# Turning and moving feed-forward blocks off TensorE in a streaming-encoder block: VectorE 32x32 turns plus transfers

## The chip, the cores and the metric

The kernel runs on one core of one Trainium2 chip. The metric is the device time of one execution in microseconds (us). Three executions of the kernel before took 1131.97, 1132.44 and 1132.74 us, median 1132.44 us. Engines are called by their names in the profile: PE (TensorE matmul), PEld (TensorE weight load), DVE (VectorE), ACT (ScalarE), POOL (GpSimd), SP (SyncE, which issues most transfers).

## What is computed

One layer of a hybrid encoder on 256 tokens of width 2048, all float32: a retention group and a state-space group side by side, an output projection added to the residual, and a dense feed-forward block of inner width 5632.

```python
h = rmsnorm(x, norm_mix_g)
proj = h @ w_in                                  # 2048 x 5120
y_ret = retention_group(q, k, v, g, ...)         # 1024 columns
y_ssm = s5_group(u, ...)                         # 1024 columns
x = x + concatenate([y_ret, y_ssm]) @ w_out      # 2048 x 2048
h = rmsnorm(x, norm_ffn_g)
x = x + (silu(h @ w_gate) * (h @ w_up)) @ w_down # 2048 x 5632, twice, and 5632 x 2048
return rmsnorm(x, norm_final_g)
```

## The kernel before, in words

**Chunks.** All weights are read from memory once, in chunks of 256 x 512 values (512 KB), numbered through the whole program: `N_IN` = 80 chunks of `w_in`, 8 of the state-space gate, 16 + 16 of `w_out` (starting at `RET0` and `SSM0`), 16 of the first `w_gate` and `w_up` column block (starting at `FFN0` = `SSM0` + 16), and then from `LOOP0` = `SSM0` + 32 on ten turns of `TURN` = 24 chunks each: 8 chunks of the next gate column block, 8 of the next up block, 8 of `w_down` for the block that the turn before computed. Nine turns are a hardware loop, the tenth is written out. A last piece works off the final `w_down` chunks.

**The pipeline of a chunk n.** SP loads it into one of four `raw` slots, once `low(n - 4)` on DVE has finished with that slot. ACT copies it to `w_hi` (`high(n)`, a rounded value that TensorE takes at full rate), once PE has finished chunk n - 4. DVE computes `w_lo = raw - w_hi` (`low(n)`). PE then multiplies three times, hi by hi, hi by lo and lo by hi, 12 matmuls of 512 columns (`column_chunk`). So `raw` and `w_hi`/`w_lo` each hold four chunks, and DVE and ACT run up to four chunks ahead of PE. Each engine's order is written out by hand: after `low(n)` or `high(n)` an engine runs what `side(n)` lists for that n, and what `turn` lists for chunk c of a turn (c from 4 to 27 on ACT and DVE, since they are four ahead, 0 to 23 on PE and SP).

**Activations must be turned.** The left operand of each matmul has its contraction index on the partitions, while results have tokens there. So two kinds of data are turned by 128x128 blocks. In both, PE turned eight blocks into PSUM at a time, ACT copied them out as the hi part, DVE computed the lo part.

- The residual `x2`, in four column blocks c of 512 (`h2_transposes(c)` on PE after chunk `SSM0 + 5 + 4c`, `h2_high(c)` and `h2_low(c)` at `SSM0 + 9 + 4c`). A column block is complete when `out_col_ssm(c)` has run on DVE at `SSM0 + 7 + 4c`; the semaphore `cols_added` says so, and PE waits for it before it turns the block.
- The feed-forward block `ff_act` (256 tokens x 512), eleven of them. `ff(count, ...)` on DVE makes it at c = 19 of a turn, for use in the next turn; `ff_transposes` on PE turned it after c = 7, `ffT_high` on ACT and `ffT_low` on DVE at c = 11; the `w_down` chunks, c = 16 to 23, use it. The eleventh block is turned near the end by the same function, into `ffE`.

**Other waits in a turn.** `down_col(0)` on DVE, at c = 21, adds the first 512 output columns to `x2` and raises `cols_added`; PE's chunk c = 20 waits for it, since it reuses those PSUM banks. `silu` on ACT, at c = 11, overwrites `ff_act`.

Of the kernel before, what the change touches and what calls it, by code (L numbers as in the profile page):

```python
# [28 lines left out]
P = 128  # L29
# [97 lines left out]
SQUARES_AT = 8  # L127

# [6 lines left out]
ACT_PART = slice(0, 768)  # L135


def build(nc, A, out):
# [20 lines left out]
    with ctx:  # L159
# [18 lines left out]
        m = overlay([("qT", [P, HEADS, SEQ], F32)], [("u_tok", [P, TOK, 1024], F32)],  # L178
                    [("cosA", [P, HALF, NCH], F32), ("sinA", [P, HALF, NCH], F32)])
        qT, u_tok, cosA, sinA = m["qT"], m["u_tok"], m["cosA"], m["sinA"]  # L180
        ret = qT
        m = overlay([("u_loc", [P, GROUPS, NCH], F32)],
                    [("ffE_hi", [P, 4, SEQ], F32R), ("ffE_lo", [P, 4, SEQ], F32R)])
        u_loc, ffE_hi, ffE_lo = (m[k] for k in ("u_loc", "ffE_hi", "ffE_lo"))
        m = overlay(
# [91 lines left out]
            "ffT_mm ffT_hi_ready ffT_lo_ready fin_sq gain_done fin_ready fin1_ready last_mm"  # L277
        ).split()
        S = {n: sem(n) for n in names}
# [66 lines left out]
        def _(sp):  # L346
            def load(n, src, turn=None):
# [8 lines left out]
                sp.dma_start((raw4 if glu else raw2)[:, slot], src).then_inc(d_raw[slot], 16)  # L356

# [39 lines left out]
            for n in range(LOOP0):  # L397
                before(n)
                if n:
                    load(n, chunk_source(n))  # L400

            sp.wait_ge(S["ret_ready"], 2)
            sp.dma_start(g_final[:], A["g_final"]).then_inc(d_gfin, 16)
            with sp.Fori(0, FG - 1) as j:
                for c in range(TURN):
# [7 lines left out]
                    load(LOOP0 + c, src.rearrange("(b p) n -> p b n", p=P), turn=j)  # L413
            for c in range(GRP):
# [11 lines left out]
        def _(act):  # L426
# [63 lines left out]
            def side(n):  # L490
# [143 lines left out]

                c, r = divmod(n - (SSM0 + 9), 4)
                if r == 0 and 0 <= c < 4:
                    h2_high(c)
                    x2_square(c)
# [41 lines left out]
            def h2_high(c):  # L680
                act.wait_ge(S["h2_mm"], c + 1)
                for k in range(4):
                    kb = 4 * c + k
                    src = ps[:, 4 + 2 * (c % 2) + k // 2, SEQ * (k % 2):SEQ * (k % 2 + 1)]
                    nc.scalar.activation(h2(kb, 0), src, ACT.Copy, scale=vec[:, V_FFN + kb:V_FFN + kb + 1]
# [73 lines left out]
        def _(dve):  # L759
# [300 lines left out]
            def h2_low(c):  # L1060
                for k in range(4):
# [3 lines left out]
                    src = ps[:, 4 + 2 * (c % 2) + k // 2, SEQ * (k % 2):SEQ * (k % 2 + 1)]  # L1065
                    gain_low(h2(kb, 1), src, V_FFN + kb, h2(kb, 0)).then_inc(S["h2_lo"], 1)
# [44 lines left out]
            def side(n):  # L1111
# [287 lines left out]
        def _(pe):  # L1399
# [252 lines left out]
            def side(n):  # L1652
# [32 lines left out]
                if r == 0 and 0 <= c < 4:  # L1685
# [63 lines left out]
            def turn(j, final=False):  # L1749
                for c in range(TURN):  # L1750
# [132 lines left out]
```

## Time and profile before

| What | Value |
|---|---|
| median of three runs | 1132.44 us |
| the profiled execution, its time | 1131.68 us |
| its span, first to last instruction | 1129.9 us |
| granted TensorE clock, mean | 0.998 |
| PE busy | 1116.9 us (99%) |
| DVE busy | 714.4 us (63%) |
| ACT busy | 532.6 us (47%) |
| transfers | 224.81 MB, mean 199 GB/s |

The profiled execution's time is 1.8 us above its span, and 0.76 us below the median of the three runs. Busy shares are means over a program whose first third (projection, retention, state space) is more crowded on DVE than the feed-forward part, which begins at about 391 us and is a regular stream of chunks.

### The profile page before, as it was taken

Reading aid. Unit: us, or ns where it says so; the run is one execution under the profiler, and the core shown is the slowest. Engines: PE = TensorE matmul, PEld = TensorE weight load, DVE = VectorE, ACT = ScalarE, POOL = GpSimd, SP = SyncE. Lnnn points to the kernel's source line nnn. Section 1 sums busy time; section 2 is a strip of 40 time slices with the busy share of each in tenths; the row PEclk is TensorE's granted clock in tenths of the full one; section 3 lists DMA queues with packets and bytes.
Section 4 is the critical chain, followed back from the end, with each engine's and each line's share of the span. In section 5 each row is a group of like instructions: output and inputs, shape, how many; then the busy total and the mean of one; then the engine's idle time right before and its main releaser. Section 6 shows DMA issues by size and latency. Waiting matters only on the chain.

```text
span 1129.9 us, 15159 instructions
## 1 busy us (share of the span) xinstructions
PE 1116.9 (99%) x5618; PEld 925.9 (82%) x5618; DVE 714.4 (63%) x783; ACT 532.6 (47%) x640; POOL 88.3 (8%) x130
## 2 busy tenths in 40 slices
PE   9999999999999999999999999999999999999996
PEld 7878778888988888888888888888888888888885
DVE  7999998566765645464555546455554645556466
ACT  7569444346734553444343343444444343443443
POOL 7120234320000000000000000000000000000000
PEclk9999999999999999999999999999999999999999
DMA  9883788855666576666665666666566666656652
GB/s 362 286 234 115 205 249 257 230 170 153 232 212 197 171 219 201 189 190 186 192 197 186 189 190 195 187 189 195 187 192 186 192 190 193 188 186 201 187 187 93
DMA packets 115095, 224.81 MB, mean 199 GB/s; under 512 B 8432, under 2 KB 13936, under 8 KB 114416
## 3 DMA queue, kind: packets, MB, share of 16 engines
q1 hardware_dynamic: 110832, 214.05, 61.1%
q0 software_dynamic: 3808, 9.31, 3.3%
q10 hardware_dynamic: 416, 0.92, 0.2%
q8 instruction: 26, 0.43, 0.2%
q14 instruction: 13, 0.11, 0.0%
HBM read 218.09 MB, written 5.11 MB: 198 GB/s over the span
## 4 chain that ended last, share of the span: by engine, by line
PE 84%; DVE 10%; DMA 2%; issue 1%; ACT 1%; POOL 0%; SPq 0%; POOLq 0%; DVEq 0%; ACTq 0%
PE ps L1415 70%; DVE w_lo L778 4%; PE ps L1440 3%; PE ps L1433 3%; PE ps L1437 3%; DMA raw<-in_w_in 2%; PE ps L1649 1%; DVE wb L905 1%; DVE wb L903 1%; DVE wb_t L904 1%; PE ps L1718 1%; PE ps L1719 1%; PE ps L1720 1%; PE ps L1548 0%; DVE cl_t L978 0%
## 5 line engine op out<-in xcount | busy, mean ns | idle before, releaser
L778 DVE TENSOR_TENSOR w_lo<-raw,w_hi 128x1024 fp32r<-128x1024 f32 x384 | 468.0, 1224 | 383.4 <-ACT w_hi L442 382.3
L442 ACT ACTIVATE w_hi<-raw 128x1024 fp32r<-128x1024 f32 x383 | 406.0, 1061 | 563.2 <-PE ps L1415 456.2
L1415 PE MATMUL ps<-w_hi,actA_hi 128*128 128x512 f32 x416 | 112.4, 392 | 0.0
L1415 PE MATMUL ps<-w_hi,actA_lo 128*128 128x512 f32 x416 | 111.2, 389 | 0.0
L1415 PE MATMUL ps<-w_lo,actA_hi 128*128 128x512 f32 x416 | 111.2, 389 | 0.0
L1415 PE MATMUL ps<-w_lo,h2B_hi 128*128 128x512 f32 x352 | 94.1, 389 | 0.0
L1415 PE MATMUL ps<-w_hi,h2B_hi 128*128 128x512 f32 x352 | 94.1, 389 | 0.0
L1415 PE MATMUL ps<-w_hi,h2B_lo 128*128 128x512 f32 x352 | 94.1, 389 | 0.0
L1415 PEld LDWEIGHTS ps<-w_hi,actA_lo 128*128 128x128 f32 x416 | 78.1, 188 | 16.3
L1415 PEld LDWEIGHTS ps<-w_lo,actA_hi 128*128 128x128 f32 x416 | 78.1, 188 | 16.2
L1415 PEld LDWEIGHTS ps<-w_hi,actA_hi 128*128 128x128 f32 x416 | 77.1, 188 | 15.3
L1415 PE MATMUL ps<-w_hi,ffT_hi 128*128 128x512 f32 x320 | 85.6, 389 | 0.0
L1415 PE MATMUL ps<-w_lo,ffT_hi 128*128 128x512 f32 x320 | 85.5, 389 | 0.0
L1415 PE MATMUL ps<-w_hi,ffT_lo 128*128 128x512 f32 x320 | 85.5, 389 | 0.0
L1415 PEld LDWEIGHTS ps<-w_hi,h2B_hi 128*128 128x128 f32 x352 | 66.1, 188 | 13.7
L1415 PEld LDWEIGHTS ps<-w_hi,h2B_lo 128*128 128x128 f32 x352 | 66.1, 188 | 13.7
L1415 PEld LDWEIGHTS ps<-w_lo,h2B_hi 128*128 128x128 f32 x352 | 66.1, 188 | 13.7
L1415 PEld LDWEIGHTS ps<-w_hi,ffT_lo 128*128 128x128 f32 x320 | 60.1, 188 | 12.5
L1415 PEld LDWEIGHTS ps<-w_lo,ffT_hi 128*128 128x128 f32 x320 | 60.1, 188 | 12.5
L1415 PEld LDWEIGHTS ps<-w_hi,ffT_hi 128*128 128x128 f32 x320 | 60.0, 188 | 12.4
L1381 POOL TENSOR_TENSOR ss<-ss 128x2 f32<-128x2 f32 x1 | 0.2, 193 | 711.4 <-ACT y1T L746 711.4
L1109 DVE TENSOR_TENSOR x<-ps,x 128x1024 f32<-128x1024 f32 x40 | 48.7, 1218 | 0.0
(271 smaller groups left out, 1265.0 us busy)
## 6 DMA issues: line engine op xcount, KB each, us to landing
raw<-in_w_gate SPq DMA_DIRECT2D x88, 512.0 KB, 3.7
raw<-in_w_up SPq DMA_DIRECT2D x88, 512.0 KB, 3.7
raw<-in_w_down SPq DMA_DIRECT2D x88, 512.0 KB, 3.7
raw<-in_w_in SPq DMA_DIRECT2D x79, 512.0 KB, 5.3
raw<-in_w_out SPq DMA_DIRECT2D x32, 512.0 KB, 3.9
k_tab<-k_scratch POOLq DMA_DIRECT2D x64, 64.0 KB, 4.3
raw<-in_ssm_w_glu SPq DMA_DIRECT2D x8, 512.0 KB, 3.6
x_tok<-in_x_tok SPq DMA_DIRECT2D x2, 1024.0 KB, 8.4
```

What stands on the lines that cost most here:

```text
L442: nc.scalar.activation(w_hi[:, s % SPL], raw[:, s % RAW], ACT.Copy).then_inc(S["high_done"], 1)
L778: tt(w_lo[:, s % SPL], raw[:, s % RAW], w_hi[:, s % SPL].bitcast(F32), ALU.subtract).then_inc(S["low_done"], 1)
L903: tt(o, of_groups(b_re, b, LOC - 1), of_powers(pr, b, 1, LOC - 1), ALU.mult)
L904: link(tt(t, of_groups(b_im, b, LOC - 1), of_powers(pi, b, 1, LOC - 1), ALU.mult))
L905: tt(o, o, t, ALU.add).then_inc(S["wb_ready"], 1)
L1109: tt(cols, ps[:, b0:b0 + 2], cols, ALU.add).then_inc(S["cols_added"], 1)
L1415: ins = mm(ps[:, banks + t], blocks[k][kind == 1][:, tok], w[:, s, at], start=first and kind == 0 and k == 0, stop=last and kind == 2 and ...
L1433: mm(ps[:, banks + t], blocks[k][0][:, tok], w_hi[:, s, at], start=first and k == 0, stop=False)
L1437: mm(ps[:, banks + t], blocks[k][1][:, tok], w_hi[:, s, at], start=False, stop=False)
L1440: ins = mm(ps[:, banks + t], blocks[k][0][:, tok], w_lo[:, s, at], start=False, stop=last and k == 1)
L1649: ins = tr(ps[:, bank + k // 2, at:at + P], ff_act[:, t, P * k:P * (k + 1)], ident[:])
L1718: mm(o, w_hi[:, n % SPL, at], hi, start=first, stop=False)
```

## The change

Twelve of the fifteen sets of eight PE turns are replaced: the ten `ff_transposes(j + 1)` inside the turns, and `h2_transposes(0)` and `(1)`. The last feed-forward block and residual columns 2 and 3 stay on PE. In the replaced cases DVE turns each 32x32 square in place (`turned_blocks`, two instructions of 128x512, one per 128 tokens, into `ff_turned` or `x2_turned`), and SP then issues sixteen transfers, one per pair (a, b) of 32-partition groups, each 32 partitions x 2 x 128 values (32 KB), which put the squares where a full turn has them (`ff_moved`, `x2_moved`). ACT and DVE read these buffers instead of PSUM. In a turn the sixteen transfers go out in pairs behind the loads of c = 5 to 12; for a residual column in groups of 6, 5 and 5 behind the loads of `SSM0 + 11 + 4c` and the next two.

Times in the order change with it: `ffT_high` moves from c = 11 to c = 15, `ffT_low` from c = 11 to c = 16, `turn_blocks` is new at c = 20, and `h2_high`/`h2_low` of the four columns go from `SSM0` + 9, 13, 17, 21 to `SSM0` + 14, 18, 18, 21.

```diff
+MOVED = 16 * 16
+COLS_MOVED = 2
+PAIRS = [(a, b) for a in range(4) for b in range(4)]
+H2_AT = (SSM0 + 14, SSM0 + 18, SSM0 + 18, SSM0 + 21)
...
+            def move(pairs, turned, moved, landed):
+
+                for a, b in pairs:
+                    sp.dma_start(moved[32 * b:32 * b + 32, :, a].rearrange("p t k j -> p t (k j)"),
+                                 turned[32 * a:32 * a + 32, b].rearrange("p t k j -> p t (k j)")).then_inc(landed, 16)
...
+                c, r = divmod(n - (SSM0 + 11), 4)
+                if 0 <= c < COLS_MOVED and r < 3:
+                    if r == 0:
+                        sp.wait_ge(S["turned"], c + 1)
+                    move(PAIRS[(0, 6, 11)[r]:(6, 11, 16)[r]], col_turned[c % 2], col_moved[c % 2], d_cols[c])
...
+                    if 5 <= c < 13:
+
+                        if c == 5:
+                            sp.wait_ge(S["turned"], j + (COLS_MOVED + 1))
+                        move(PAIRS[2 * (c - 5):2 * (c - 4)], ff_turned, ff_moved, d_moved)
...
             def h2_high(c):
-                act.wait_ge(S["h2_mm"], c + 1)
+                if c < COLS_MOVED:
+                    act.wait_ge(d_cols[c], MOVED)
+                else:
+                    act.wait_ge(S["h2_mm"], c + 1 - COLS_MOVED)
...
             def ffT_high(count):
-                act.wait_ge(S["ffT_mm"], count)
-                nc.scalar.activation(ffT_hi[:].rearrange("p (a b) s -> p a (b s)", a=2), ps[:, 4:6], ACT.Copy
+                act.wait_ge(d_moved, count * MOVED)
+                nc.scalar.activation(turned_view(ffT_hi[:]), moved_view, ACT.Copy
                                      ).then_inc(S["ffT_hi_ready"], 1)
...
                     if c == GRP + SPL - 1:
+
+                        act.wait_ge(S["turned"], j + (COLS_MOVED + 1))
+                        silu(j * TURN + (LOOP0 + GRP))
+                    if c == GRP + SPL + 3:
                         ffT_high(j + 1)
-                        silu(j * TURN + (LOOP0 + GRP))
...
+            def turn_blocks(count, moved):
+
+                dve.wait_ge(S["ff_ready"], count)
+                if moved is not None:
+                    dve.wait_ge(d_moved, moved)
+                else:
+                    dve.wait_ge(d_cols[2 * (COLS_MOVED - 2)], MOVED)
+                turned_blocks(ff_turned, ff_act)
...
+            def turned_blocks(to, x):
+
+                for t in range(TOK):
+                    last = nc.vector.transpose(to[:, :, t].rearrange("p b k j -> p k b j"),
+                                               x[:, t].rearrange("p (k b j) -> p k b j", k=4, b=4))
+                last.then_inc(S["turned"], 1)
...
+                    if not last and c == 2 * GRP + 4:
+                        turn_blocks(j + 2, (j + 1) * MOVED)
...
-                if r == 0 and 0 <= c < 4:
+                if r == 0 and COLS_MOVED <= c < 4:
                     h2_transposes(c)
...
                         pe.wait_ge(S["cols_added"], j * 4 + 8)
-                        ff_transposes(j + 1)
```

**Place 1, DVE around the residual columns.** `x` in the rows is `x2`; the L1085 rows (with the change L1135) are `out_col_ssm(2)` and `out_col_ssm(3)`, the L778 rows (L828) are `low`, the L792 rows (L842) are `h2_low`. Before, from `out_col_ssm(2)` at `SSM0 + 15` to `out_col_ssm(3)` at `SSM0 + 19`:

```order
L1085 SCALAR_TENSOR_TENSOR x<-ps,rstd,x 128x512 x2
L778 TENSOR_TENSOR w_lo<-raw,w_hi 128x1024 x2
L792 SCALAR_TENSOR_TENSOR h2B_lo<-ps,x_in,h2B_hi 128x256 x4
L778 TENSOR_TENSOR w_lo<-raw,w_hi 128x1024 x2
L1085 SCALAR_TENSOR_TENSOR x<-ps,rstd,x 128x512 x2
```

With the change, from `h2_low(0)` at `SSM0 + 14` to `low(SSM0 + 21)`:

```order
L842 SCALAR_TENSOR_TENSOR actA_lo<-ff_moved,x_in,actA_hi 128x256 x4
L828 TENSOR_TENSOR w_lo<-raw,w_hi 128x1024
L1135 SCALAR_TENSOR_TENSOR x<-ps,rstd,x 128x512 x2
L828 TENSOR_TENSOR w_lo<-raw,w_hi 128x1024 x3
L842 SCALAR_TENSOR_TENSOR actA_lo<-x_moved,x_in,actA_hi 128x256 x4
L842 SCALAR_TENSOR_TENSOR h2B_lo<-ps,x_in,h2B_hi 128x256 x4
L828 TENSOR_TENSOR w_lo<-raw,w_hi 128x1024
L1135 SCALAR_TENSOR_TENSOR x<-ps,rstd,x 128x512 x2
L828 TENSOR_TENSOR w_lo<-raw,w_hi 128x1024 x2
```

Between `low(SSM0 + 18)` and `out_col_ssm(3)` there now stand eight small instructions and one `low`, where there was one `low`: column 1's lo part came here from `SSM0 + 13`, column 2's from `SSM0 + 17`.

**Place 2, DVE inside the loop, c = 19 to 21 of a turn.** Before:

```order
L778 TENSOR_TENSOR w_lo<-raw,w_hi 128x1024
L1091 ISA
L1093 SCALAR_TENSOR_TENSOR ff_act<-ps,rstd,ff_act 128x512 x2
L777 REGISTER_ALU
L778 TENSOR_TENSOR w_lo<-raw,w_hi 128x1024
L777 REGISTER_ALU
L778 TENSOR_TENSOR w_lo<-raw,w_hi 128x1024
L1106 ISA
L1109 TENSOR_TENSOR x<-ps,x 128x2x512
```

With the change:

```order
L828 TENSOR_TENSOR w_lo<-raw,w_hi 128x1024
L1141 ISA
L1143 SCALAR_TENSOR_TENSOR ff_act<-ps,rstd,ff_act 128x512 x2
L827 REGISTER_ALU
L828 TENSOR_TENSOR w_lo<-raw,w_hi 128x1024
L1150 REGISTER_ALU
L1168 STREAM_TRANSPOSE ff_turned<-ff_act 128x4x4x32 x2
L827 REGISTER_ALU
L828 TENSOR_TENSOR w_lo<-raw,w_hi 128x1024
L1181 ISA
L1184 TENSOR_TENSOR x<-ps,x 128x2x512
```

The two block turns stand between the `low` of c = 20 and that of c = 21, ahead of `down_col(0)` (L1109, now L1184), for which PE waits.

**Place 3, SP's queue at the residual columns.** Before, the rows are 31 loads of `w_out` and 8 of `w_gate` with nothing between. With the change:

```order
L383 DMA raw<-in_w_out 128x2x512 x27
L388 DMA ff_moved<-ff_turned 32x2x128 x6
L383 DMA raw<-in_w_out 128x2x512
L388 DMA ff_moved<-ff_turned 32x2x128 x5
L383 DMA raw<-in_w_out 128x2x512
L388 DMA ff_moved<-ff_turned 32x2x128 x5
L383 DMA raw<-in_w_out 128x2x512 x2
L388 DMA x_moved<-x_turned 32x2x128 x6
L383 DMA raw<-in_w_gate 128x2x512
L388 DMA x_moved<-x_turned 32x2x128 x5
L383 DMA raw<-in_w_gate 128x2x512
L388 DMA x_moved<-x_turned 32x2x128 x5
```

Thirty-two small transfers now stand in the one queue that also issues the weight loads, and the first of each sixteen waits for DVE's turns.

## Rows read from the trace of the kernel before

**Rows 1.** The page: span, and busy time of the engines.

```profile
span 1129.9 us, 15159 instructions
...
PE 1116.9 (99%) x5618; PEld 925.9 (82%) x5618; DVE 714.4 (63%) x783; ACT 532.6 (47%) x640; POOL 88.3 (8%) x130
```

**Rows 2.** Waits, whole span: who waited for whom, total us, times, longest.

```profile
ACT w_hi L442 <- PE ps L1415: 456.2, 283, 2.6
DVE w_lo L778 <- ACT w_hi L442: 382.3, 305, 4.8
```

**Rows 3.** The chain that ended last: start us, us, engine, line, instructions.

```profile
374.36 10.90 PE ps L1415 x48
386.13 10.90 PE ps L1415 x48
397.91 59.86 PE ps L1415 x264
458.64 65.30 PE ps L1415 x288
...
1054.20 35.38 PE ps L1415 x156
```

**Rows 4.** Windows, one turn: PE, PEld, DVE, ACT, POOL busy; clock, DMA share, GB/s.

```profile
657.16:723.33 66.17, 66.17 (x297) 54.88 (x297) 36.42 (x31) 27.53 (x28) 0.00 (x0) 1.00 0.63 190
```

**Rows 5.** Groups by form, DVE: line, operation, shapes, count, busy us, mean ns.

```profile
L1093 DVE SCALAR_TENSOR_TENSOR ff_act<-ps,rstd,ff_act 128x512 f32<-128x512 f32 x22 | 15.4, 743 | 0.0
...
L1246 DVE TENSOR_SCALAR x_gain<-x_gain,rstd 128x512 f32<-128x512 f32 x2 | 0.9, 480 | 0.0
...
L946 DVE TENSOR_TENSOR_SCAN state<-decays,state 128x1024 f32<-128x1024 f32 x2 | 4.6, 2292 | 0.1
```

**Rows 6.** Timeline, first turn, c = 19 to 21: DVE, and PEld at chunk 20.

```profile
482.69 1.40 DVE L1093 SCALAR_TENSOR_TENSOR ff_act<-ps,rstd,ff_act 128x512 f32<-128x512 f32 x2
484.27 1.22 DVE L778 TENSOR_TENSOR w_lo<-raw,w_hi 128x1024 fp32r<-128x1024 f32 x1 [0.18 <-ACT w_hi L442]
486.99 1.23 DVE L778 TENSOR_TENSOR w_lo<-raw,w_hi 128x1024 fp32r<-128x1024 f32 x1 [1.49 <-ACT w_hi L442]
488.13 1.22 DVE L1109 TENSOR_TENSOR x<-ps,x 128x1024 f32<-128x1024 f32 x1
...
490.91 0.87 PEld L1415 LDWEIGHTS ps<-w_hi,ffT_hi 128*128 128x128 f32 x4
```

**Rows 7.** Timeline, residual columns, from chunk SSM0 + 17 on: ACT, DVE, PEld.

```profile
385.36 1.06 ACT L442 ACTIVATE w_hi<-raw 128x1024 fp32r<-128x1024 f32 x1 [1.66 <-PE ps L1415]
386.32 1.55 ACT L685 ACTIVATE h2B_hi<-ps,x_in 128x256 fp32r<-128x256 f32 x4
387.75 0.64 ACT L694 ACTIVATE sqT<-x 128x512 f32<-128x512 f32 x1
...
387.59 1.65 DVE L792 SCALAR_TENSOR_TENSOR h2B_lo<-ps,x_in,h2B_hi 128x256 fp32r<-128x256 f32 x4
...
393.92 1.40 DVE L1085 SCALAR_TENSOR_TENSOR x<-ps,rstd,x 128x512 f32<-128x512 f32 x2
...
396.64 1.02 PEld L1641 LDWEIGHTS ps<-ident,x 128*128 128x128 f32 x8
```

**Rows 8.** SP's issues (ns min/median/max), and landing times in 420 to 460 us.

```profile
L356 SPq DMA_DIRECT2D raw<-in_w_gate x88: 367/373/388, 373.2 to 1034.1; - x88
...
L375 SPq DMA_DIRECT2D ident<-in_ident x1: 468/468/468, 17.6 to 17.6; - x1
...
raw<-in_w_gate SPq DMA_DIRECT2D x8, 512.0 KB, 4.5
```

**Rows 9.** Timeline, first turn: `ff(1)`, `high(LOOP0 + 6)`, and PE at that chunk.

```profile
438.33 1.41 DVE L1093 SCALAR_TENSOR_TENSOR ff_act<-ps,rstd,ff_act 128x512 f32<-128x512 f32 x2
...
444.20 1.06 ACT L442 ACTIVATE w_hi<-raw 128x1024 fp32r<-128x1024 f32 x1 [1.66 <-PE ps L1415]
...
452.16 1.07 PE L1415 MATMUL ps<-w_hi,h2B_hi 128*128 128x512 f32 x4
```

More of the change, by code:

```diff
@@ L276, in build @@
             "zT_ready sqT_ready ssm_hi ssm_lo sq_added ssq_mm ssq_ready cols_added last_added h2_mm h2_hi h2_lo x2_sq silu_ready ff_ready "
-            "ffT_mm ffT_hi_ready ffT_lo_ready fin_sq gain_done fin_ready fin1_ready last_mm"
+            "turned ffT_mm ffT_hi_ready ffT_lo_ready fin_sq gain_done fin_ready fin1_ready last_mm"
         ).split()
+        d_moved = sem("d_moved")
+        d_cols = [sem(f"d_cols{i}") for i in range(COLS_MOVED)]
         S = {n: sem(n) for n in names}
@@ L339, in y_half, with turned_col, col_block, turned_view @@
             return slice(2 * P * (b % 2), 2 * P * (b % 2 + 1))
+        def turned_col(c, k):
+            if c < COLS_MOVED:
+                return col_moved[c % 2][:].rearrange("p t a k j -> p (t a) k j")[:, :, k]
+            return ps[:, 4 + 2 * (c % 2) + k // 2, SEQ * (k % 2):SEQ * (k % 2 + 1)]
+        def col_block(x, c):
+            return x.rearrange("p (b j) -> p b j", j=32) if c < COLS_MOVED else x
+        moved_view = ff_moved[:].rearrange("p t a k j -> p (t a) k j")
+        def turned_view(x):
+            return x.rearrange("p k (c j) -> p c k j", j=32)
         def flat(x):
@@ L633, in side @@
                         glu_half(p // 2)
+                for c in range(4):
+                    if n == H2_AT[c]:
+                        h2_high(c)
                 c, r = divmod(n - (SSM0 + 9), 4)
                 if r == 0 and 0 <= c < 4:
-                    h2_high(c)
                     x2_square(c)
@@ L680, in h2_high @@
             def h2_high(c):
-                act.wait_ge(S["h2_mm"], c + 1)
+                if c < COLS_MOVED:
+                    act.wait_ge(d_cols[c], MOVED)
+                else:
+                    act.wait_ge(S["h2_mm"], c + 1 - COLS_MOVED)
                 for k in range(4):
                     kb = 4 * c + k
-                    src = ps[:, 4 + 2 * (c % 2) + k // 2, SEQ * (k % 2):SEQ * (k % 2 + 1)]
-                    nc.scalar.activation(h2(kb, 0), src, ACT.Copy, scale=vec[:, V_FFN + kb:V_FFN + kb + 1]
+                    nc.scalar.activation(col_block(h2(kb, 0), c), turned_col(c, k), ACT.Copy, scale=vec[:, V_FFN + kb:V_FFN + kb + 1]
                                          ).then_inc(S["h2_hi"], 1)
@@ L1173, in side @@
                     out_col_ssm(c - 4)
-                c, r = divmod(n - (SSM0 + 9), 4)
-                if r == 0 and 0 <= c < 4:
-                    h2_low(c)
+                    if c - 4 < COLS_MOVED:
+                        turn_column(c - 4)
+                for c in range(4):
+                    if n == H2_AT[c]:
+                        h2_low(c)
                 if n == LOOP0 + 3:
                     ff(1, LOOP0)
+                    turn_blocks(1, None)
             for n in range(LOOP0 + SPL):
```

33 lines of the change are left out of this document (19 added, 14 removed).

## The prediction

> **What bounds the kernel now.** I read the page first: TensorE is busy 99% of the span [rows 1]. That alone does not say that its work is the limit, so I read the waits next. ACT's largest wait, 456 us in 283 times, is for PE to free a weight slot, and DVE's is for ACT [rows 2]. The helpers wait for PE, not PE for them. The chain of work that ended last says the same and gives the price of the work in question. From 391 us on it is pieces of PE matmuls and nothing else. A turn of the loop is one piece of 288 matmuls, 65.30 us, and the pieces start (1054.20 - 458.64) / 9 = 66.17 us apart [rows 3]. The 0.87 us between two pieces is the set of eight turns on the identity. For a residual column, 386.13 - 374.36 - 10.90 = 0.87 as well [rows 3]. A matmul takes 59.86 / 264 = 0.2267 us, so a chunk of twelve takes 2.72 us [rows 3]. In that time DVE is busy 36.4 of 66.2 us and ACT 27.5, and transfers take 0.63 of their engines [rows 4]. The granted clock there is 1.00, the 2.4 GHz level, with PE never idle [rows 4].
>
> **What is removed.** Ten sets in the turns and two at the residual columns, at 0.87 each: 12 x 0.873 = **10.5 us off PE**, all of it on the path.
>
> The Trainium skill, page "VectorE: DVE Perf Modes", section "The three transpose paths", gives 390 ns for a 128x128 turn on TensorE; eight of them would be 3.1 us and twelve sets 37 us, by that page. The trace has 0.87 us for eight, so the trace's number is used. The same page's rules tell authors to turn 128x128 blocks on TensorE where PSUM will do, which speaks against this change; the trace shows TensorE as the full engine here, so I do not follow it.
>
> **Block turns on DVE.** Two instructions of 128x512 per set, an operation the trace doesn't have. Call one X. The nearest rows of that size are 0.48 us (one source) and 0.74 us (two sources, one in PSUM); the slowest one at this density is the scan, 2.29 us for 1024, so 1.15 for 512 [rows 5]. One pass over 512 values with scattered writes is nearest to the plain rows: I take X = 0.70, with 0.48 to 1.15 as ends.
>
> That same page gives 311 ns for a 128x128 on VectorE, so by an estimate from it X = 4 x 0.311 = 1.24 us; the sum below would be the same.
>
> The place where X can reach PE is c = 20 and 21 of a turn. `low` of c = 20 hands over at about 485.41 (1.14 after 484.27, the step seen from 486.99 to 488.13), and `low` of c = 21 starts at 486.99, so 1.58 us are empty. `down_col(0)` ends at 489.35 and PE's chunk 20, which waits for it, loads its weights at 490.91: another 1.56 us [rows 6]. Two block turns therefore cost nothing up to 2X = 3.1 us, X = 1.57. With 2X = 1.4 they fit into the gap even without the second reserve, and at 2.3 they use half of it. Behind them on DVE stand only `low` 21 and `down_col(0)`. `ffT_low` moves to c = 16, three chunks before PE needs it, (8.16 - 3.5) some 4.7 us of reserve.
>
> **Transfers.** SP issues a load in 0.37 us and a 64 KB one in 0.47 [rows 8]. Sixteen at 0.47 are 7.5 us per set. In a turn two go behind each load: 0.37 + 0.94 = 1.3 us of 2.72, free. The last is issued when PE is at about c = 5; ACT asks for it behind `high(15)`, when PE is at c = 12. That leaves more than 12 us after a landing of 4.5 us, so that wait never shows. In bytes the moves add 0.5 MB to 12.6 MB a turn (share 0.63 to 0.66); by pieces, 1024 of 512 bytes more to 6144 of 2 KB (to 0.73 at the cost per packet of [rows 4]). Neither end fills the transfers.
>
> What the waits of SP do to the loads behind them matters more. A load is issued when `low(n - 4)` ends, 2.3 us after PE frees chunk n - 8, and PE needs the result seven chunks later: 19.0 - 2.3 - 4.5 (landing) - 2.3 (`high` and `low`) = **9.9 us by which a load may be late** [rows 3, 8]. Three places use it. (a) Each residual column: SP stands until `out_col_ssm(c)` and the turns are done, 1.4 + 2X = 2.8 us, and then 16 moves and 4 loads take 9.0 us of the 10.9 that four chunks last, so loads are 2.8 us late and recover. (b) The first turn: SP waits at c = 5 for the first `turn_blocks`, which comes only after `ff(1)` (to 439.8) and 2X, so 441.2, plus 0.9 for two moves. The load of LOOP0 + 6 goes out at 442.2 instead of 435.6. It lands at about 447.2 (0.5 more for the moves ahead of it), `high` and `low` end at 449.4, and PE takes that chunk at 452.2 [rows 9]. `high` is late by 3 us, PE by nothing, with 2.8 us left. (c) Later turns: the turned block is ready before the turn starts. No stop.
>
> **The residual columns.** Column 0's squares: from `low(7)`, 2.8 + 8.3 (issues) + 4.5 = 15.6 us, against 17.7 until ACT asks at `SSM0 + 14`. That holds, and column 1 follows the same pattern. The tight place is `SSM0 + 18`, where columns 1 and 2 are both split. In the clock of the trace before: `high(18)` can start at 385.36 + 0.87 + 2.72 = 388.95, and is passed on after 0.96. Eight activations, 1.43 per four (386.32 to 387.75), last to 392.8. `high(19)` comes then, and DVE may take it at 393.9. DVE meanwhile does `low(18)` (390.05 to 391.2), two `h2_low` at 1.6 each (1.65 with the tail) to 394.4, `low(19)` to 395.5, and `out_col_ssm(3)` at 1.40 to 396.9. Before, that ended at 395.3. PE's turns of column 3 wait for it and load weights at 396.64 [rows 7]. So **about 0.3 us of PE stall, once** (0 to 0.6, as the steps add up). Every matmul behind it waits with it; `low(20)` has a reserve of several us.
>
> **The sum.** The profiled execution took 1131.68 us (span 1129.9). -10.5 + 0.3 = -10.2: 1121.5, span 1119.7. The median of the runs lies 0.76 above the profiled execution, so the median becomes **1122.3 us**, 0.9% faster. The first part of the program, to about 358 us, and the tail are the same instructions.
>
> **Rivals.**
>
> *Block turns are slow on float32.* If X is above 1.57, `down_col(0)` is late in each of the nine turns that hold a `turn_blocks`, and PE waits 9 x (2X - 3.1). The gain is gone at 2X = 4.25, X = 2.1. At X = 2.3, twice the scan's pace, it is 9 x 1.5 = 13.5 us: 1135.8 us, slower. For it: the operation is not in the trace, and it writes 32-value pieces. Against: no DVE row is above 1.15 us per 512 columns [rows 5]. Chance 0.06, of it slower than before 0.05.
>
> *SP's queue falls behind.* If one small transfer costs SP 1.0 us, the two residual columns take 17.5 us per 10.9, 13 us late for both, plus 2.8. That is 6 us over the 9.9: about 1128 us. In the turns 2.4 us still fit in 2.72. For it: one queue carries everything, and each transfer reads and writes only 32 partitions. Against: SP's issues vary only from 0.37 to 0.47 with shape [rows 8]. A milder form, landings of 8 us and more behind the moves, ends at 1123 to 1126. Chance 0.08.
>
> *PE's time was not the limit.* If the weight stream or the helpers set 2.72 us per chunk, removing PE work leaves 1132.4. Against it stand the 1.66 us that ACT waits for PE in every chunk [rows 7, 9] and a chain of PE alone. Chance 0.04.
>
> **How the numbers follow.** Forecast 0.82, slow turns 0.06, queue 0.08, not the limit 0.04. A change within 0.2% (2.3 us) is about what this measurement can't tell from none. Forecast and queue are both faster, and so is the mild end of slow turns: faster 0.91. Same 0.04, slower 0.05. The forecast's own range is 1121 to 1123.5 (stall 0 to 0.6, gap 0.87, spread of runs 0.8). The range of 8 in 10 takes in the milder queue case: 1120.8 to 1125.
>
> **What would show it.** The 65.30 us pieces should repeat every 65.3 us instead of 66.17. The identity turns should number 24 on the residual and last block, with STREAM_TRANSPOSE at 0.5 to 1.2 us. ACT's wait for d_moved should not appear. PE should show one idle piece under 0.6 us before the turns of column 3, and SP one stop of about 4 us at the first turn. Wrong would be: PE idle before chunk 20 of each turn (slow turns), or ACT waiting for `raw` transfers around 360 to 400 or 445 us (queue).

## The result

The kernel with the change took 1125.43 us (median of 5 runs, 1124.87 to 1127.45), beside 1132.44 us for the kernel before (5 runs on the same chip, 1131.71 to 1132.74). The ratio is 0.9942, with an interval of 0.9928 to 0.9957. It is faster, as forecast, but by 7.0 us instead of 10.1: 3.1 us above the forecast, and 0.4 us above the upper end of the range.

The profiled execution took 1125.43 us. The page of it, span and busy times:

```profile
span 1123.6 us, 15221 instructions
...
PE 1106.7 (98%) x5522; PEld 915.7 (81%) x5522; DVE 728.3 (65%) x807; ACT 533.3 (47%) x640; POOL 88.4 (8%) x130
```

Against [rows 1], PE has lost 96 instructions (twelve sets of eight) and 10.2 us of busy time. The span has lost only 6.3 us, so PE must now stand somewhere. The waits, over the whole span, say where (who waited for whom, total, times, longest):

```profile
ACT w_hi L485 <- PE ps L1495: 430.3, 272, 4.3
...
ACT w_hi L485 <- DMA raw<-in_w_out: 11.0, 5, 2.7
...
PEld ps L1718 <- DVE x L1135: 4.2, 2, 2.2
PE ps L1718 <- DVE x L1135: 3.4, 2, 1.8
```

The first row answers to [rows 2]: ACT still waits mostly for PE. The others are the residual columns. ACT waits for weights to land (`raw<-in_w_out`), and PE waits twice, 3.4 us in all, for `out_col_ssm` on DVE (L1135) before it turns columns 2 and 3 (L1718). The chain that ended last is the second witness:

```profile
326.76 38.26 PE ps L1495 x168
...
366.20 1.24 DVE w_lo L828
...
367.90 0.59 SPq L388
...
374.94 4.30 DMA raw<-in_w_out
...
386.90 0.60 SPq L388
...
387.55 3.91 DMA raw<-in_w_gate
...
392.57 1.23 DVE w_lo L828
393.80 1.58 DVE actA_lo L842 x4
...
400.56 682.75 PE ps L1495 x3012
```

Before, it was PE alone from 326 us on, in pieces with 0.87 us between them; [rows 3] has these pieces from 374 us on. Now the whole loop and the chunks around it are one piece: 682.75 / 3012 = 0.2267 us per matmul, the same rate, without a gap. From 365 to 400 us, though, the chain leaves PE. From 367.90 to 374.90 it runs through ten of SP's small transfers (L388) and one load in a row, then through a weight load, ACT and DVE; from 384.36 to 387.50 it runs through five more, and then again through a weight load, ACT and DVE.

**How the chain is to be read.** SP's timeline of that stretch has the cause (start, us, instructions, in SP's own order). Residual column 0 uses the buffers `ff_turned` and `ff_moved`, which the feed-forward blocks need only later, and column 1 uses `x2_turned` and `x2_moved`, `x_turned` and `x_moved` in the rows:

```profile
361.95 5.27 SPq L388 DMA_DIRECT2D ff_moved<-ff_turned  x6
367.27 0.59 SPq L383 DMA_DIRECT2D raw<-in_w_out  x1
367.90 3.14 SPq L388 DMA_DIRECT2D ff_moved<-ff_turned  x5
371.08 0.59 SPq L383 DMA_DIRECT2D raw<-in_w_out  x1
371.71 3.19 SPq L388 DMA_DIRECT2D ff_moved<-ff_turned  x5
374.94 1.10 SPq L383 DMA_DIRECT2D raw<-in_w_out  x2
376.09 3.79 SPq L388 DMA_DIRECT2D x_moved<-x_turned  x6
...
384.36 3.14 SPq L388 DMA_DIRECT2D x_moved<-x_turned  x5
387.55 10.94 SPq L383 DMA_DIRECT2D raw<-in_w_gate  x6
```

The rows for L383 are the loads of `SSM0` + 12, + 13, and + 14 with + 15; the last begins with the load of `SSM0` + 18. The one of + 14 goes out at 374.94, though `low(SSM0 + 10)`, which frees its slot, ends at 366.20 + 1.23 = 367.43 (first row of the next fence). It is 7.5 us late. One issue of the first six took 1.93 us where the others took 0.60, and 1.3 of the 7.5 us are due to it. ACT, DVE and PEld behind it, from their timelines (an idle time and its releaser in brackets):

```profile
366.20 1.23 DVE L828 TENSOR_TENSOR w_lo<-raw,w_hi 128x1024 fp32r<-128x1024 f32 x1 [1.49 <-ACT w_hi L485]
...
379.27 1.06 ACT L485 ACTIVATE w_hi<-raw 128x1024 fp32r<-128x1024 f32 x1 [1.71 <-DMA raw<-in_w_out]
...
380.36 1.22 DVE L828 TENSOR_TENSOR w_lo<-raw,w_hi 128x1024 fp32r<-128x1024 f32 x1 [2.91 <-ACT w_hi L485]
381.51 1.66 DVE L842 SCALAR_TENSOR_TENSOR actA_lo<-ff_moved,x_in,actA_hi 128x256 fp32r<-128x256 f32 x4
383.09 1.22 DVE L828 TENSOR_TENSOR w_lo<-raw,w_hi 128x1024 fp32r<-128x1024 f32 x1
384.22 1.40 DVE L1135 SCALAR_TENSOR_TENSOR x<-ps,rstd,x 128x512 f32<-128x512 f32 x2
...
385.68 0.86 PEld L1718 LDWEIGHTS ps<-ident,x 128*128 128x128 f32 x8 [2.05 <-DVE x L1135]
...
399.46 0.86 PEld L1718 LDWEIGHTS ps<-ident,x 128*128 128x128 f32 x8 [2.20 <-DVE x L1135]
```

(`actA_lo<-ff_moved` is column 0's lo part.) The load lands at 379.24 and `high(SSM0 + 14)` starts at once. DVE then has `low(14)`, column 0's lo part, `low(15)` and only then `out_col_ssm(2)`, without a pause. PE would have turned column 2 at 383.6; it gets the column at 385.68. The weights that are late are not the ones PE waits for.

### The profile page after: what moved, and what is told of

The parts are those of the page before. It is cut to its first block, busy times and chain, and to the rows that moved or that the text cites. A ratio compares the mean times of both kernels' runs of the same rounds, so it can differ in the third digit from the quotient of the medians.

```text
span 1123.6 us, 15221 instructions
## 1 busy us (share of the span) xinstructions
PE 1106.7 (98%) x5522; PEld 915.7 (81%) x5522; DVE 728.3 (65%) x807; ACT 533.3 (47%) x640; POOL 88.4 (8%) x130
## 4 chain that ended last, share of the span: by engine, by line
PE 81%; DVE 11%; DMA 3%; issue 2%; ACT 1%; SPq 1%; POOL 0%; POOLq 0%; DVEq 0%; ACTq 0%
PE ps L1495 68%; DVE w_lo L828 4%; PE ps L1520 3%; PE ps L1513 3%; PE ps L1517 3%; DMA raw<-in_w_in 2%; SPq L388 1%; ACT w_hi L485 1%; DVE wb L955 1%; DVE wb L953 1%; DVE wb_t L954 1%; PE ps L1795 1%; PE ps L1797 1%; PE ps L1796 1%; PE ps L1628 0%
## 5 line engine op out<-in xcount | busy, mean ns | idle before, releaser
L828 DVE TENSOR_TENSOR w_lo<-raw,w_hi 128x1024 fp32r<-128x1024 f32 x384 | 467.6, 1223 | 362.7 <-ACT w_hi L485 362.0
L1184 DVE TENSOR_TENSOR x<-ps,x 128x1024 f32<-128x1024 f32 x40 | 48.7, 1217 | 0.0
```

The costliest lines, as they stand in the source:

```text
L828: tt(w_lo[:, s % SPL], raw[:, s % RAW], w_hi[:, s % SPL].bitcast(F32), ALU.subtract).then_inc(S["low_done"], 1)
L1184: tt(cols, ps[:, b0:b0 + 2], cols, ALU.add).then_inc(S["cols_added"], 1)
```

## The experiments

The theory: SP's issues of the 32 small transfers make the weight loads late, and a late load holds up `out_col_ssm` in DVE's order. The rivals: it is DVE's new work and order alone; it is SP's standing for the turned squares, not the issuing; part of the loss lies in the turns of the loop. There are three groups of runs (a, b and c), each on one chip with its own runs of the kernel before. Beside the medians this table has two things from the profiled execution: PEld's stops in 380 to 400 us, and the time from the start of a piece of 108 matmuls, which every trace has, to the end of the span. Its row in the chain is, before and with the change:

```profile
300.89 24.51 PE ps L1415 x108
...
301.47 24.51 PE ps L1495 x108
```

The part ahead of that piece differs by up to 0.9 us from one trace to the next and is no part of the change, so this time compares more finely than the span.

| Kernel | median us (runs) | ratio to before, interval | PEld stops us | piece to end us |
|---|---|---|---|---|
| before | 1132.44 (5) | 1 | none | 829.0 |
| the change | 1125.43 (5) | 0.9942, 0.9928 to 0.9957 | 2.05, 2.20 | 822.1 |
| a1_ff_only | 1123.16 (5) | 0.992, 0.9907 to 0.9934 | none | 820.0 |
| a2_cols_only | 1134.09 (11) | 1.0021, 1.0012 to 1.003 | 1.93, 2.16 | 830.9 |
| a3_cols_pool | 1124.08 (5) | 0.993, 0.9917 to 0.9944 | 0.34 | 820.4 |
| a4_turn_only | 1121.65 (4) | 0.9908, 0.9893 to 0.9924 | 0.35 | 818.4 |
| b1_order | 1122.72 (5) | 0.9917, 0.9903 to 0.9931 | 0.53, 0.72 | 819.4 |
| b2_spread | 1123.0 (5) | 0.9917, 0.9904 to 0.9931 | 1.23 | 819.4 |
| b3_moves_only | 1122.75 (5) | 0.9922, 0.9908 to 0.9935 | 1.37 | 819.4 |
| b4_pool_extra | 1125.08 (4) | 0.9938, 0.9923 to 0.9953 | none | 822.0 |
| c1_spread_order | 1121.85 (4) | 0.9906, 0.9891 to 0.9921 | 0.69 | 818.7 |
| c2_dual | 1121.78 (4) | 0.9905, 0.989 to 0.992 | none | 818.3 |
| c3_after_again | 1125.19 (5) | 0.994, 0.9926 to 0.9954 | 1.52, 2.49 | 821.9 |

The kernel before had medians of 1132.33 (15 runs), 1132.04 (9) and 1132.57 us (9) beside the groups a, b and c.

**a1_ff_only: the ten blocks in the turns alone.**

```diff
-COLS_MOVED = 2
+COLS_MOVED = 0
...
-H2_AT = (SSM0 + 14, SSM0 + 18, SSM0 + 18, SSM0 + 21)
+H2_AT = (SSM0 + 9, SSM0 + 13, SSM0 + 17, SSM0 + 21)
...
```

> Only the ten feed-forward blocks are turned by VectorE and moved; all four residual columns stay on TensorE, in the order of the kernel before. Theory A (the two TensorE stops of 2.1 and 2.2 us come only from the residual columns' transfers in SP's queue): the full 10 x 0.873 = 8.7 us are gained, 1123.7 us, and TensorE shows no idle piece in the residual columns or in the turns. Rival B (part of the loss sits in the turns, as longer pieces or stops there): 1124.5 or more, with pieces of more than 65.3 us per turn.

1123.16 us, where 1123.7 was expected. Ten sets give 829.0 - 820.0 = 9.0 us, 0.90 each, and nothing is lost in the turns. With fewer blocks moved, the kernel is 2.3 us faster than the whole change.

**a2_cols_only: columns 0 and 1 alone.** The ten blocks go back to PE.

```diff
-                    if 5 <= c < 13:
...
-                        move(PAIRS[2 * (c - 5):2 * (c - 4)], ff_turned, ff_moved, d_moved)
...
+                        ff_transposes(j + 1)
```

> Only residual columns 0 and 1 are turned by VectorE and moved; all feed-forward blocks stay on TensorE. Theory A: -2 x 0.87 + 4.2 = +2.5 us, so slower than the kernel before, 1134.9 us, with the same two TensorE stops ahead of the turns of columns 2 and 3 as in the changed kernel. Rival B (the stops need the rest of the change): 1130.7 us, 1.7 us faster than before.

1134.09 us, 1.8 us slower than before in the same group (2.5 expected), with both of PEld's stops at their places:

```profile
385.40 0.86 PEld L1708 LDWEIGHTS ps<-ident,x 128*128 128x128 f32 x8 [1.93 <-DVE x L1127]
399.14 0.85 PEld L1708 LDWEIGHTS ps<-ident,x 128*128 128x128 f32 x8 [2.16 <-DVE x L1127]
```

The two parts add up: 829.0 - 9.0 + 1.9 = 821.9, and the change has 822.1. So the two parts don't disturb each other, and the columns cost 3.7 us for the 1.8 that they save (two sets at 0.90).

**a3_cols_pool: the columns' 32 transfers issued by GpSimd.**

```diff
-                    move(PAIRS[(0, 6, 11)[r]:(6, 11, 16)[r]], col_turned[c % 2], col_moved[c % 2], d_cols[c])
...
+            for c in range(COLS_MOVED):
+                pool.wait_ge(S["turned"], c + 1)
+                for a, b in PAIRS:
+                    pool.dma_start(col_moved[c][32 * b:32 * b + 32, :, a].rearrange("p t k j -> p t (k j)"),
...
```

> The changed kernel, with the 32 transfers of the residual columns issued by GpSimd on its own queue instead of by SP; the turns, the places of h2_high and h2_low and the transferred data are the same. Theory A (SP's issue time of 0.64 us per transfer holds up the weight loads): the loads go out on time again, the stop ahead of column 2 vanishes, the one ahead of column 3 falls to about 0.3 us: 1121.9 to 1122.5 us. Rival C (the traffic of the small transfers itself makes the loads land late): the stops stay above 1 us each, 1124 us or more. Rival D (VectorE's longer list, turns and two h2_low at one place): stops unchanged, 1125.4 us.

SP's queue is clear, and the loads are on time. DVE adds column 2 at 381.18, and PEld turns it without a stop; before column 3 only 0.34 us are left (ACT, DVE, and PEld in the timelines of this kernel):

```profile
376.22 1.06 ACT L480 ACTIVATE w_hi<-raw 128x1024 fp32r<-128x1024 f32 x1 [0.29 <-PE ps L1496]
...
381.18 1.40 DVE L1130 SCALAR_TENSOR_TENSOR x<-ps,rstd,x 128x512 f32<-128x512 f32 x2
...
383.90 1.02 PEld L1719 LDWEIGHTS ps<-ident,x 128*128 128x128 f32 x8
...
395.97 0.86 PEld L1719 LDWEIGHTS ps<-ident,x 128*128 128x128 f32 x8 [0.34 <-DVE x L1130]
```

These four rows give the reserves that the change had. `high(SSM0 + 14)` here starts 376.22 - 363.71 = 12.51 us after `low(SSM0 + 9)`, with the change 379.27 - 363.48 = 15.79: 3.3 us late. A load 7.5 us late thus had 7.5 - 3.3 = 4.2 us of slack before ACT noticed. DVE had 383.90 - 381.18 - 1.46 = 1.26 us (1.46 from the add's start to PEld's, as 385.68 - 384.22). And 3.3 - 1.26 = 2.0 us is the first stop. Together, then, the load could be 4.2 + 1.26 = 5.5 us late before PE stood.

But the time is 1124.08, 2 us more than the missing stops allow. The 2 us lie behind the long piece of 3012 matmuls: from its end to the end of the span it is 1122.1 - 1079.85 = 42.25 us, in a1 1121.7 - 1081.42 = 40.28. SP's waits of a3 have a longer last one, for PE's sequencer at the program's very end, behind the outputs:

```profile
SPq L165 <- PEq L165: 4.3, 1, 4.3
```

In a1 the same wait is shorter:

```profile
SPq L165 <- PEq L165: 2.3, 1, 2.3
```

b4 takes that up.

**a4_turn_only: DVE turns the columns, nothing is moved.**

```diff
-                return col_moved[c % 2][:].rearrange("p t a k j -> p (t a) k j")[:, :, k]
+                return col_turned[c % 2][:].rearrange("p b t k j -> p (b t) k j")[:, :, k]
...
-                    act.wait_ge(d_cols[c], MOVED)
+                    act.wait_ge(S["turned"], c + 1)
```

> The changed kernel without the 32 transfers of the residual columns: VectorE turns the 32x32 squares, and ScalarE and VectorE read them unmoved, so the squares of columns 0 and 1 are in the wrong places. Feed-forward blocks as in the changed kernel. Theory A and rival C: no late loads, the stop ahead of column 2 gone and 0.3 us ahead of column 3, 1122.2 us. Rival D (VectorE's order): both stops stay, 1125.4 us.

1121.65 us. The squares of columns 0 and 1 stay in the wrong places here, so this run is for its time alone. The DVE work and the new order are all there, and the stop before column 3 is 0.35 us. The transfers, and what they do to SP, are the whole of the loss beyond these 0.35: 822.1 - 818.4 = 3.7 us.

**b1_order: column 0's parts behind `low(SSM0 + 15)` instead of ahead of it.**

```diff
-H2_AT = (SSM0 + 14, SSM0 + 18, SSM0 + 18, SSM0 + 21)
+H2_AT = (SSM0 + 15, SSM0 + 19, SSM0 + 19, SSM0 + 21)
```

> The changed kernel with h2_high and h2_low of columns 0 to 3 at SSM0 + 15, 19, 19 and 21 instead of 14, 18, 18 and 21. The four instructions of h2_low(0) and the eight of columns 1 and 2 then stand on VectorE behind out_col_ssm(2) and out_col_ssm(3), for which TensorE waits, not ahead of them; SP's queue is as in the changed kernel, and the loads are as late. Theory A (the stops are late weight loads plus what stands ahead of out_col_ssm on VectorE): the first stop shrinks by 1.6 us to about 0.5, the second vanishes or stays below 0.5: 1121.7 us. Rival C (late loads alone are enough, whatever the order on VectorE): less than 1 us gained, 1124.5 us or more.

SP's queue is untouched, and the loads are nearly as late: the one of `SSM0 + 14` goes out at 374.11, 6.75 us after its slot came free (367.36). The 0.8 us less come from the issues of the first group, whose longest took 0.95 us here instead of 1.93. With a reserve of 5.5 us (from a3) that would still be a stop of some 1.3 us in the change's order. Yet the first stop is gone, since `out_col_ssm(2)` now stands ahead of the 1.6 us of column 0's lo part. The second shrinks to 0.53 (it was expected to vanish or stay below 0.5). A new one of 0.72 comes right behind it: column 1's lo part is now too late for chunk `SSM0 + 18`, which is the first to use it.

```profile
395.86 0.86 PEld L1718 LDWEIGHTS ps<-ident,x 128*128 128x128 f32 x8 [0.53 <-DVE x L1135]
397.44 0.77 PEld L1495 LDWEIGHTS ps<-w_hi,actA_hi 128*128 128x128 f32 x4 [0.72 <-DVE actA_lo L842]
```

**b2_spread: the sixteen transfers as 4, 4, 4, 4 behind four loads.**

```diff
-                if 0 <= c < COLS_MOVED and r < 3:
+                if 0 <= c < COLS_MOVED:
...
-                    move(PAIRS[(0, 6, 11)[r]:(6, 11, 16)[r]], col_turned[c % 2], col_moved[c % 2], d_cols[c])
+                    move(PAIRS[4 * r:4 * r + 4], col_turned[c % 2], col_moved[c % 2], d_cols[c])
```

> The changed kernel with the sixteen transfers of a residual column in groups of 4, 4, 4 and 4 behind four loads instead of 6, 5 and 5 behind three; nothing else is moved. Theory A, at 0.64 us per transfer: a load's interval on SP becomes 3.2 us instead of 4.5 and 3.8, the load of SSM0 + 14 is 4 us late instead of 7.5 and the first stop vanishes; but SP now has no free load in which to catch up, loads SSM0 + 18 and 19 are 6 us late and the second stop stays near 2 us: 1123.4 us. Rival D (VectorE's order alone makes the stops): no change, 1125.4 us.

The first stop is gone here too, with the same 32 transfers; the load of `SSM0 + 14` is 4.4 us late (371.50 against 367.10). The second stays at 1.23, where near 2 was expected. Two rows of SP's timeline show why it stays:

```profile
378.48 2.50 SPq L388 DMA_DIRECT2D x_moved<-x_turned  x4
381.03 0.59 SPq L383 DMA_DIRECT2D raw<-in_w_gate  x1
```

Four transfers and a load take 3.18 us (381.66 - 378.48), and a chunk lasts 2.72. Over eight chunks SP falls 3.7 us behind, so one even spacing doesn't cure the second column.

**b3_moves_only: the transfers, without DVE's turns and without SP's wait for them.** They read another buffer, so that columns 0 and 1 hold other data; this run too is for its time alone.

```diff
-                    if r == 0:
-                        sp.wait_ge(S["turned"], c + 1)
-                    move(PAIRS[(0, 6, 11)[r]:(6, 11, 16)[r]], col_turned[c % 2], col_moved[c % 2], d_cols[c])
...
+                    for a, b in PAIRS[(0, 6, 11)[r]:(6, 11, 16)[r]]:
+                        sp.dma_start(col_moved[c % 2][32 * b:32 * b + 32, :, a].rearrange("p t k j -> p t (k j)"),
+                                     zT[32 * a:32 * a + 32, 2 * b:2 * b + 2, 0:P]).then_inc(d_cols[c], 16)
...
```

> The changed kernel without VectorE's turns of residual columns 0 and 1 and without SP's wait for them: the 32 transfers are issued at the same places in SP's queue, but from another buffer that is long complete, so columns 0 and 1 of the turned residual hold other data. It separates SP's standing for the turns (2.7 us a column) from its issue time. Theory A: by issue time alone load SSM0 + 14 is 4 us late, not 7.5, so the first stop vanishes; for column 1 the lateness adds up to 7 or 8 us and a second stop of 1.5 to 2.5 us stays: 1123.5 us. Rival E (the standing alone makes the loads late): both stops vanish but for 0.3 us, 1122 us.

Without the turns and the 2.3 us that SP stands for them, the load of `SSM0 + 14` is only 4.6 us late (372.03 against 367.45) and the first stop vanishes; the second is still 1.37. That DVE's turns are gone as well doesn't matter to these loads: the `low` of `SSM0 + 9`, + 10 and + 11 start within 0.02 us of their times with the change. The median, 1122.75, lies between what issuing alone (1123.5) and what standing alone (1122) should give, and so do the stops: standing and issuing together are needed for the first stop, and issuing without the standing leaves 1.37 of the 2.20 us of the second.

**b4_pool_extra: a1 with 32 transfers on GpSimd's queue that nothing in the columns needs.**

```diff
+            for i in range(2):
+                for a, b in PAIRS:
+                    to = (col_moved[1][32 * b:32 * b + 32, :, a], col_turned[1][32 * b:32 * b + 32, a])[i]
+                    pool.dma_start(to.rearrange("p t k j -> p t (k j)"),
+                                   zT[32 * a:32 * a + 32, 2 * b:2 * b + 2, 0:P]).then_inc(d_extra, 16)
```

> The kernel with the ten feed-forward blocks alone moved (1123.2 us), plus 32 transfers of 32 KB that GpSimd issues at the residual columns between two buffers that nobody uses then. In the kernel where GpSimd issued the column transfers, the last output transfer was issued 3.5 us earlier than in the changed kernel, yet the span ended only 1.5 us earlier: the end of the program took 2 us longer. Theory F (each transfer on GpSimd's queue costs at the program's end): SP's last wait grows from 2.3 to 4.3 us and the time to 1125.2 us. Rival G (it was something else in that kernel's end): 1123.2 us and a last wait of 2.3 us.

PE has no stop at the columns, and its part of the chain is a1's. The last wait is 4.3 us again instead of a1's 2.3, and the time from the piece to the end is 822.0 instead of 820.0. The part behind the piece of 3012 matmuls is 1122.8 - 1080.60 = 42.2 us, as in a3. So 32 transfers issued by GpSimd cost 1.9 us when the program ends, though nobody waits for them at that place. What happens there the traces don't show.

**c1_spread_order: 4, 4, 4, 4, and column 0 at `SSM0 + 15`, 1 at + 18, 2 at + 19.** The edits are those of b2 and this one:

```diff
+H2_AT = (SSM0 + 15, SSM0 + 18, SSM0 + 19, SSM0 + 21)
```

> Both repairs together: column transfers in groups of 4, 4, 4 and 4, and h2_high/h2_low of columns 0 to 3 at SSM0 + 15, 18, 19 and 21, so that out_col_ssm(2) has nothing but low ahead of it and out_col_ssm(3) only h2_low(1). Theory A: no first stop, second stop 0 to 0.3 us, and column 1 is ready for SSM0 + 18, where the kernel with the order alone had a stop of 0.7: span 1119.6, 1121.3 us. Against it: each repair alone already gave 2.7 us, and if there is a loss that neither touches, the two together stay at 1122.5.

1121.85 us, one stop of 0.69, ahead of column 3, where 0 to 0.3 was expected and 1121.3 us. It beats the kernel before by 0.94% and the change (c3) by 3.3 us on the same chip.

**c2_dual: the same order, half of the transfers issued by ACT.** SP issues two behind each of four loads, ACT the other two.

```diff
+                    for a, b in PAIRS[8 + 2 * r:10 + 2 * r]:
+                        act.dma_start(col_moved[c % 2][32 * b:32 * b + 32, :, a].rearrange("p t k j -> p t (k j)"),
...
```

> As c1_spread_order, but each column's sixteen transfers are issued half by SP (two behind each of four loads) and half by ScalarE (two behind each of four high). SP then needs 1.9 us per chunk and is late only by its 2.7 us wait, so the loads are on time, at the price of 1.3 us of ScalarE time in each of eight chunks, where it is idle for 1.66. Theory A: no stop at all, 1121.0 us, within 0.3 of c1_spread_order. Rival H (ScalarE's issues make high late where TensorE needs it): a stop behind high(SSM0 + 13) or (SSM0 + 17), where the squares stand too, 1122 us or more.

No stop at all, as the two rows of PEld show:

```profile
383.69 1.02 PEld L1726 LDWEIGHTS ps<-ident,x 128*128 128x128 f32 x8
...
395.47 1.02 PEld L1726 LDWEIGHTS ps<-ident,x 128*128 128x128 f32 x8
```

The profile has what no stops should give: 829.0 - 818.3 = 10.7 us, 0.89 for each of twelve sets. Its median, 1121.78, can't be told from c1's. That is the change without its loss, and the forecast without its stall. The median is 0.8 us above the 1121.0 that was expected of it.

**c3_after_again: the change itself, beside c1 and c2.**

> The changed kernel again, unaltered, beside the two repairs on the same chip: 1125.4 us and the same two stops of about 2 us. One of its transfers took SP 1.9 us to issue in the first trace (the others 0.6); if that is a chance event that moves from run to run, the first stop should differ by up to 1 us between traces.

The first stop is 1.52 here, 0.53 less than before, and the longest issue of its first six took 1.55 us instead of 1.93: the load of `SSM0 + 14` is 7.1 us late instead of 7.5 (374.35 against 367.27). So the stop does move with that one issue from trace to trace. The second stop is 2.49.

1125.19 us: the 3.3 and 3.4 us to c1 and c2 are no difference between chips. The intervals of the ratios don't touch.

## Why the prediction was right, and where it failed

**What bounds, and what is removed: right.** 10.5 us predicted for twelve sets; c2 shows 10.7. No transfer limit and no helper limit appeared.

**Block turns on DVE: right.** X was taken as 0.70, with no place in the turns where it would be felt. It measured 0.69 (ns min/median/max of the feed-forward blocks' turns, then first and last start). No row of the operation stood behind the 0.70, so the close hit is in part luck; by the prediction's own working anything up to 1.57 would have given the same time:

```profile
L1168 DVE STREAM_TRANSPOSE ff_turned<-ff_act x20: 668/687/711, 442.4 to 1010.0; 128x512 f32<-128x512 f32 x20
```

The estimate from the Trainium skill's page "VectorE: DVE Perf Modes", section "The three transpose paths", was 1.24 us; the trace shows little more than half of it. (The figures of that section are for 128x128 in bf16, these blocks are float32. Its 390 ns for a turn on TensorE would be 3.1 us for eight, where the traces show 0.87 to 0.90.) At c = 20 and 21 of the first turn (DVE, then PEld at chunk 20), against [rows 6]:

```profile
487.18 1.30 DVE L1168 STREAM_TRANSPOSE ff_turned<-ff_act 128x512 f32<-128x512 f32 x2
...
488.76 1.23 DVE L828 TENSOR_TENSOR w_lo<-raw,w_hi 128x1024 fp32r<-128x1024 f32 x1 [0.28 <-ACT w_hi L485]
489.90 1.22 DVE L1184 TENSOR_TENSOR x<-ps,x 128x1024 f32<-128x1024 f32 x1
...
492.68 0.87 PEld L1495 LDWEIGHTS ps<-w_hi,ffT_hi 128*128 128x128 f32 x4
```

The two turns lie in the gap, `low` of c = 21 still has 0.28 us to wait for ACT, and between `down_col(0)`'s end and PE there are 492.68 - 491.12 = 1.56 us, the same as before.

**The turns' transfers: right.** Share of the transfers, last but one column, in one period of 65.30 us, against [rows 4]:

```profile
640.00:705.30 65.30, 65.30 (x290) 54.06 (x289) 37.63 (x33) 27.59 (x28) 0.00 (x0) 1.00 0.69 201
```

0.69 lies between the predicted 0.66 and 0.73. No wait of ACT for `d_moved` appears. The issues were mis-sized here too, without harm: in the first turn a load and two transfers take 1.9 us of SP (445.29 to 447.23, two transfers 1.24) instead of 1.3, of the 2.72 that a chunk lasts. The first turn went as told in its effect on PE: SP stands for the turned block (9.8 us in two waits, of which 2.3 at residual column 0), shown by its waits:

```profile
SPq L388 <- DVE ff_turned L1168: 9.8, 2, 7.5
```

The prediction's list of signs has this stop at about 4 us; 7.5 were measured. Its own times give about 8 (block ready at 441.2, the load before issued by 435.6 - 2.72 + 0.37 = 433.3), so the sign was a slip.

Behind it the load of `LOOP0 + 6` is late, ACT's `high` comes at 449.54, where the rhythm of 2.72 us from the one before (444.14) would have it at 446.86. It is 2.7 us late (predicted 3), and PE doesn't notice:

```profile
444.14 1.06 ACT L485 ACTIVATE w_hi<-raw 128x1024 fp32r<-128x1024 f32 x1 [1.66 <-PE ps L1495]
449.54 1.06 ACT L485 ACTIVATE w_hi<-raw 128x1024 fp32r<-128x1024 f32 x1 [4.34 <-PE ps L1495]
```

(The profile puts this wait down to PE, which had been done for long; it was the transfer.)

**The residual columns' stall by order: right.** "About 0.3 us of PE stall, once": 0.34 and 0.35 in a3 and a4, where SP's queue is out of it.

**Step that failed, first: "Sixteen at 0.47 are 7.5 us per set."** SP's issues:

```profile
L388 SPq DMA_DIRECT2D ff_moved<-ff_turned x16: 586/596/1932, 362.0 to 374.3; - x16
L388 SPq DMA_DIRECT2D x_moved<-x_turned x16: 585/597/597, 376.1 to 386.9; - x16
```

0.60 us each, and 0.04 between two (3.79 us for six): 10.2 us per set. The loads among them took 0.59 instead of 0.37. Sixteen and four loads are then 16 x 0.64 + 4 x 0.63 = 12.8 us per 10.9 us of four chunks, not 9.0; the first set took 376.09 - 361.95 = 14.1, as one issue was 1.9. So "loads are 2.8 us late and recover" was wrong: the load of `SSM0 + 14` was 7.5 us late, and the one of `SSM0 + 18`, right behind the 32nd transfer, still 6.0 (387.55, its slot free at 380.36 + 1.22 = 381.58). The row taken, a 64 KB load of the identity at 0.47 [rows 8], is one of 128 partitions; the bound above it (1.0, in the rival) was noted but without a step in between. Nor was it so that "SP's issues vary only from 0.37 to 0.47 with shape": in the trace before, single loads of `x_in` at the program's start took SP 0.77 us (at 2.11) and 0.63 us (at 4.42).

**Step that failed, second: "9.9 us by which a load may be late."** That is the reserve until PE needs this chunk's own weights. It held: PE never waited for weights here. But DVE works in order, and behind `low(SSM0 + 14)` stood `out_col_ssm(2)`, which PE needs ahead of its own chunk `SSM0 + 14`, for the turns of column 2. The reserve on that way was 4.2 us until ACT notices and 1.26 on DVE, 5.5 in all. With 7.5 us it was overrun by 2.0. The same reserve fits the other traces with this order on DVE, by how late the load of `SSM0 + 14` was: 4.4 us (b2) and 4.6 (b3) gave no first stop, 7.1 (c3) gave 1.52 and 7.5 gave 2.05. Place 1 of the change's order had the row; I walked it for column 3 with loads on time, but never with late ones.

Either error alone would have been harmless at the first stop: 7.5 us of lateness is less than the 9.9 believed in, and the 2.8 us believed in are less than 5.5. One part of the lateness nothing in the prediction could tell: 1.3 of the 7.5 us are the single long issue. Without it the load would be 6.2 us late and the first stop, by an estimate from the same reserve, 0.7 us. The runs agree that it takes both: with the standing gone (b3), the load spread (b2) or the order relaxed (b1), the first stop disappears. The second is the same mechanism one column later, with `SSM0 + 18`, where both columns' parts lie in the way.

**Where the 3.1 us went.** The medians differ by 7.0 us; c2, without stops, has 10.8 beside its own runs of the kernel before. The difference is 3.8. PE's own two waits are 3.4 us, and 822.1 - 818.3 is 3.8. Forecast were 10.5 and a stall of 0.3. By the finer measure the forecast is 829.0 - 10.2 = 818.8, and 822.1 is 3.3 above it: 3.8 of stops, less the 0.3 that were forecast, less the 0.2 by which twelve sets gave more than 10.5. The 0.4 us between PE's waits and the 3.8, and that 0.2, I have not traced further.

**The rivals.** Slow turns: no. PE not the limit: no. The queue rival (0.08 in both forms) came true in its cause and not in either of its sizes: the queue did fall behind by what a small transfer costs SP, at 0.60 us instead of the 1.0 of the strong form. The time lies where the mild form put it ("ends at 1123 to 1126"), but not by its mechanism, landings of 8 us and more: the transfers landed in 2.6 us median here, and at most in 4.4. By the prediction's own reserve of 9.9, issues of 0.60 would have cost nothing.

## What to carry to other kernels

A transfer has a price on the queue that issues it, and one of 32 KB cost more of it here (0.60 us) than a load of 512 KB (0.37): count it per instruction, from a row of the same shape or with a range where there is none, and against the time that the queue's other customers leave. When an instruction becomes late, don't take the reserve of its own consumer: go down the in-order queue behind it and take the smallest reserve found there. Undoing the change part by part shows which part pays: here two of twelve replaced sets took 1.9 us more than they gave, and an even spread with two places of the order moved made them a gain of 1.3 us (c1 against a1: 820.0 - 818.7).

## What the hardware showed unexpectedly

A transfer of 32 partitions x 2 x 128 values, 32 KB, held SP for 0.60 us, more than a 512 KB load of 128 partitions (0.37), and ACT for 0.59 to 0.73 in c2; the longest idle time that ACT shows behind such an issue is 0.33 us. Loads issued among such transfers took 0.59 in the straight-line part. Issued by GpSimd (a3: 16 in 8.5 us), they took 0.53 each and left TensorE's work alone, but 32 of them made the program's end 2.0 us longer, a3 and b4 alike (42.2 us behind the long piece instead of 40.3). Single issues of the same form on SP took 1.93 us in the profile of the change, 1.55 in c3 and 1.25 in c2, and a load 1.75 in c1, without a cause that the traces show.
